# PEER selection of the dense tokens stretched over the first products, and gathered rows of v 128 rounds behind those of u instead of 40

## What is computed

```python
q = (xb @ w_q).reshape(blk, PEER_HEADS, 2, PEER_HALF)          # 8 heads, two halves of 128
s = jnp.einsum('thcd,hcnd->thcn', q, sub_keys)                 # 128 keys for each half
s_top, i_top = lax.top_k(s, PEER_TOPK)                         # 16 best of each half
cand_s = (s_top[:, :, 0, :, None] + s_top[:, :, 1, None, :])   # 256 pairs
best_s, best_pos = lax.top_k(cand_s, PEER_TOPK)                # 16 best pairs = 16 experts
expert = jnp.take_along_axis(cand_e, best_pos, axis=-1)        # of 128 * 128
gate = jax.nn.softmax(best_s, axis=-1)
act = jax.nn.gelu(jnp.einsum('td,thkd->thk', xb, u[expert]))
return jnp.einsum('thk,thkd->td', gate * act, v[expert])
```

## Time and profile before

| what | us |
|---|---|
| runs of the kernel | 5276.35 median of 3 (5275.28 to 5283.59) |
| the profiled execution | 5254.98 |
| its span in the trace | 5253.1 |
| PEER of layer 0, gathers 1044 to 2476, first stage until | 1843 |
| its one-hot stage | 1843 to 1996 |
| its third stage, with the last gathers | 1996 to 2476 |
| PEER of layer 1, first stage until | 4585 |

### The profile page before, as it was taken

The page is one execution under the profiler, slowest core; times in us unless marked ns, Lnnn a source line. Parts: engine busy times, 40 slices in busy tenths (PEclk is TensorE's granted clock), DMA queues, the critical chain, the costliest instruction groups (busy, mean ns, idle before and its releaser), DMA issues. The chain is left out here.

```text
span 5253.1 us, 56097 instructions
## 1 busy us (share of the span) xinstructions
PE 4308.1 (82%) x21158; PEld 3533.7 (67%) x21158; DVE 3096.9 (59%) x5685; ACT 1026.1 (20%) x2272; POOL 1920.2 (37%) x1559
## 2 busy tenths in 40 slices
PE   6989679788997559996787799996888997469995
PEld 5467438577886458885555688863677886458884
DVE  1315540599957796656216633345599867796656
ACT  0102310222332150000012222211222332150000
POOL 0000230166657624444002433312256557614444
PEclk9985669899998779998878788858899998779997
DMA  2330112488889948998111000013588889939998
GB/s 91 89 75 1 34 37 96 167 301 313 311 338 397 369 128 342 409 396 348 56 58 35 1 1 1 1 41 104 188 300 310 319 341 390 363 109 371 409 399 333
DMA packets 403487, 1099.26 MB, mean 209 GB/s; under 512 B 70508, under 2 KB 157261, under 8 KB 402886
## 3 DMA queue, kind: packets, MB, share of 16 engines
q0 software_dynamic: 186496, 679.04, 34.4%
q1 hardware_dynamic: 216726, 416.69, 22.6%
HBM read 1066.88 MB, written 32.45 MB: 209 GB/s over the span
## 5 line engine op out<-in xcount | busy, mean ns | idle before, releaser
L1036 DVE SCALAR_TENSOR_TENSOR gg_ytok<-gg_ring,gg_gw,gg_ytok 128x1024 f32<-128x1024 f32 x320 | 422.1, 1319 | 178.5 <-DMA gg_ring<-in_peer_v,gg_idx 172.5
L1036 DVE SCALAR_TENSOR_TENSOR fg_ytok<-fg_ring,fg_gw,fg_ytok 128x1024 f32<-128x1024 f32 x320 | 422.0, 1319 | 176.6 <-DMA fg_ring<-in_peer_v,fg_idx 170.0
L706 POOL DMA_INDIRECT fg_ring<-in_peer_u,fg_idx x320 | 377.2, 1179 | 351.7 <-DVE fg_ring L1030 284.4
L706 POOL DMA_INDIRECT gg_ring<-in_peer_u,gg_idx x320 | 374.4, 1170 | 345.7 <-DVE gg_ring L1030 275.9
L1030 DVE SCALAR_TENSOR_TENSOR fg_ring<-fg_ring,fg_htok 128x1024 f32<-128x1024 f32 x320 | 409.7, 1285 | 128.1 <-DMA fg_ring<-in_peer_u,fg_idx 126.4
L1030 DVE SCALAR_TENSOR_TENSOR gg_ring<-gg_ring,gg_htok 128x1024 f32<-128x1024 f32 x320 | 409.8, 1286 | 127.8 <-DMA gg_ring<-in_peer_u,gg_idx 125.7
L774 PE MATMUL fg_bank<-f_hTd,fg_uT 128*128 128x256 f32 x2048 | 476.9, 387 | 0.6 <-ACT f_buf L873 0.6
L774 PE MATMUL gg_bank<-g_hTd,gg_uT 128*128 128x256 f32 x2048 | 476.2, 387 | 0.6 <-ACT g_buf L873 0.6
L706 POOL DMA_INDIRECT gg_ring<-in_peer_v,gg_idx x320 | 358.1, 1119 | 272.1 <-DVE gg_ytok L1036 211.8
L706 POOL DMA_INDIRECT fg_ring<-in_peer_v,fg_idx x320 | 345.7, 1080 | 276.3 <-DVE fg_ytok L1036 214.4
L774 PEld LDWEIGHTS fg_bank<-f_hTd,fg_uT 128*128 128x128 f32 x2048 | 389.8, 196 | 51.2 <-issue 0.9
(11 more groups left out here) (620 smaller groups left out, 7758.8 us busy)
## 6 DMA issues: line engine op xcount, KB each, us to landing
fg_ub<-in_peer_u SPq DMA_DIRECT2D x128, 512.0 KB, 6.8
gg_ub<-in_peer_u SPq DMA_DIRECT2D x128, 512.0 KB, 6.7
fg_ub<-in_peer_v SPq DMA_DIRECT2D x64, 512.0 KB, 7.2
fg_uT<-in_peer_v SPq DMA_DIRECT2D x64, 512.0 KB, 6.7
gg_ub<-in_peer_v SPq DMA_DIRECT2D x64, 512.0 KB, 7.3
gg_uT<-in_peer_v SPq DMA_DIRECT2D x64, 512.0 KB, 6.8
f_buf<-in_peer_w_q SPq DMA_DIRECT2D x16, 1024.0 KB, 12.2
g_buf<-in_peer_w_q SPq DMA_DIRECT2D x16, 1024.0 KB, 11.8
```

Source lines behind the costliest of these rows:

```text
L706: pool.indirect_dma_start(ring[:, n % RING, :], None, (u_rows if kind == "u" else v_rows)[:, :], bass.IndirectOffsetOnAxis(ap=idx[:, r:r + ...
L1036: dve.scalar_tensor_tensor(ytok[:, :], row, gw[:, r:r + 1], ytok[:, :], ALU.mult, ALU.add).then_inc(used, 1)
```

## The change

Passes 4 to 7, those of the dense tokens, now have 55, 55, 55 and 30 units between their steps and 18, 18, 18 and 14 blocks beside them, so that 263 of the 370 units of the first stage lie among selection steps instead of 172, and 97 of the 128 blocks instead of 65. `LAG` goes from 40 to 128 (`SLOTS`). The selection buffers are laid out in the order in which they come free, and ACT's one wait at block 79 becomes five, at blocks 79 (queries multiplied), 95 (last scores), 108, 113 and 118 (picked). The margin for the dots' Gelus goes from 25 to 40. No instruction of the computation is added or removed.

```diff
-LAG = 40
+LAG = SLOTS
-UNITS_SEL = (0, 20, 24, 24, 26, 26, 26, 26)
-BLOCKS_SEL = (3, 8, 9, 9, 9, 9, 9, 9)
+UNITS_SEL = (0, 20, 24, 24, 55, 55, 55, 30)
+BLOCKS_SEL = (3, 8, 9, 9, 18, 18, 18, 14)
-HTR_AT = 16640
+HTR_AT = 17664
...
-        for c, k in zip(early_chunks, place(sched, [dots_at[c] for c in early_chunks], 25.0)):
+        for c, k in zip(early_chunks, place(sched, [dots_at[c] for c in early_chunks], 40.0)):
...
-                        if b == lim_end:
-                            act.wait_ge(gate_done, npass)
+                        if b == lim_w:
+                            act.wait_ge(mm_done, 4 * npass)
+                        if b == lim_q:
+                            act.wait_ge(sc_done, npass)
+                        if b == lim_s:
+                            act.wait_ge(s_used, npass)
+                        if b == lim_rest:
+                            act.wait_ge(off_done, npass)
+                        if b == lim_hit:
                             act.wait_ge(idx_done, npass)
```

More of the change, by code:

```diff
@@ L474, in top_of_buf @@
             return buf[:, free[0]:free[0] + n]
+        hit = top_of_buf(10 * TOPK * TOPK).rearrange("p (a e i j) -> p a e i j", a=2, e=5, i=TOPK)
+        lim_hit = free[0] // TD
+        s_rest = top_of_buf(10 * P).rearrange("p (e c n) -> p e c n", e=5, c=2)
+        lim_rest = free[0] // TD
+        s_sb = top_of_buf(10 * P).rearrange("p (e c n) -> p e c n", e=5, c=2)
+        lim_s = free[0] // TD
+        qT = top_of_buf(4 * TR).rearrange("p (h c t) -> p h c t", h=2, c=2)
         keysT = top_of_buf(HC * P).rearrange("p (h n) -> p h n", n=P)
+        lim_q = free[0] // TD
         wt = top_of_buf(4 * D).rearrange("p (b k n) -> p b k n", b=2, k=KD)
[L478 to L482, removed]
+        lim_w = free[0] // TD
         lim_a = HTR_AT // TD
@@ L563, in peer_layer @@
             if p + 1 < npass:
+                assert nb <= lim_w, (nb, lim_w)
                 some_queries(p + 1)
@@ L567, in peer_layer @@
                 assert nb <= lim_a, (nb, lim_a)
-        assert nb <= lim_end, (nb, lim_end)
         some_blocks(nblk - nb)
```

## The result

The changed kernel took 5246.51 us (median of 4 runs, 5242.55 to 5251.9), the kernel before 5277.24 in the runs beside it (4 runs). The ratio is 0.9947, interval 0.9925 to 0.9968: faster by 31 us, more than the 10.5 us that the prediction took as what can be told from no change, and less than half of the 66 that were forecast.

The account below looks back on a forecast made before the run. DMA was taken to bind the first stage once selection is stretched; -44 + 6 + 5 = -33 us a layer, -66 for two layers, takes 5276.35 to 5210 us, range 5165 to 5262.

Parts of the forecast that it names:

- share 0.95 from the beginning of pass 4: First stage, layer f: DMA share 0.95 or more from 1217 us on would show the forecast right.
- a sign against itself: Passes of the first stage: DMA share below 0.9 would say that unused DMA time had not become used.
- The term of -44: First stage: with selection stretched, DMA binds and the stage ends at 1799 instead of 1843, 44 us less a layer.
- the lower bound of 17: First stage: gain of only 17 us if 218 MB go at 358 GB/s, taking 609 us.
- The first rival: First stage: the mix stays at the passes' rate, gains 17 us, -6 a layer after the exchange, 5264 us; chance 0.17.
- fast mix: First stage: the mix goes at the third stage's 401 GB/s, gains 82 us, 71 a layer net, 5134 us; chance 0.09.
- the full queue without holes: First stage from pass 4: 582 us of full queue at share 1.02 take 570 us, before 12 us for mask holes.
- slower: One-hot and third stages: ytok exchange costs 15 and 11 us, first stage gains at most 17; 5294 us; chance 0.05.
- No change: Selection steps: DVE waits for late scores or exponentials, 23 or 46 us a layer; within some 20 of 5276; chance 0.05.
- +6 and +5: Exchange of ytok between neighbouring units of v: DVE's stops add 6 us to the one-hot stage, 5 to the third.
- The exponential and ACT's five waits: First stage: DVE's 22.8 us wait for the last pass's exponential goes; ACT's five waits cost 0.
- the step from "DMA unused" to "DMA used": First stage: what it can gain is what its DMA leaves unused, so 582 us of full queue sets its length.

Follow-up runs that it names:

- mask cut: The changed kernel, but POOL multiplies only a sixteenth of the mask in the four dense passes, so work is left out: 5226.26 us, ratio 0.9887.
- the last experiment: Changed kernel with ring of seven, units behind all seven steps, lag 116: 5143.86 us; from it, mask halves apart: 5140.79 us; mask mostly left out: 5139.9 us.

## Why the prediction was off

*What bounds the stage.* Right for what binds afterwards: DMA share is 0.95 over the stage, DVE's waits moved into the passes, and TensorE ended 51 us ahead of DVE. Of the signs that the prediction named, share 0.95 from the beginning of pass 4 came out at 0.95 for the stage, but under 0.9 in pass 7, which it had put down as a sign against itself. TensorE took 553 us from the beginning of pass 4, 508 without its waits of 45; the prediction had 530 and 510.

*The term of -44.* This is the step that failed: "a pass still has holes ... Half of 6.53 in each of four passes is 12 us". Measured are -19.4 and -22.2, near the lower bound of 17 and not the value. The queue lay open for 42 us, and 39 of them lie in the passes (40 in layer g), as many as the 35 and 40 of before. The prediction read the open queue in the passes of before as "DVE is nearly always busy", which units moved in between would use, and counted only the stretch in which POOL works on something else, the mask. It overlooked that DVE stops freeing places whenever it carries out steps: 8.4 us at the beginning of each pass, and shorter steps between. Six gathers cover most of that but not all, and the queue then needs another ten microseconds to fill. These holes belong to the steps, and the stretch puts more units between the steps but leaves as many steps as there were. The row was at hand: in the kernel before, too, POOL stood with six gathers out at the beginning of pass 5 (first row below). What the stretch did close lies behind the passes, 22 us before and 3 after, and some 16 of these 22 are the stretch around DVE's wait for the last exponential (second row, of before).

```profile
1290.09 1.74 POOL L706 DMA_INDIRECT fg_ring<-in_peer_u,fg_idx  x1 [7.68 <-DVE fg_ring L1030]
...
1472.00:1502.00 30.00, 30.00 (x168) 26.81 (x167) 7.15 (x11) 13.05 (x25) 4.25 (x4) 1.00 0.49 154
```

After, the first 22 us of each of the four passes, and 14 us from the beginning of each product of the mask:

```profile
1236.50:1258.50 22.00, 22.00 (x122) 19.64 (x121) 18.75 (x63) 10.17 (x19) 11.96 (x10) 0.99 0.82 273
1358.40:1380.40 22.00, 22.00 (x125) 19.66 (x124) 18.96 (x59) 7.76 (x17) 11.15 (x9) 1.00 0.88 322
1474.90:1496.90 22.00, 22.00 (x123) 19.65 (x122) 19.06 (x57) 7.40 (x16) 11.59 (x10) 1.00 0.92 338
1588.80:1610.80 22.00, 22.00 (x124) 19.48 (x123) 21.79 (x83) 7.70 (x18) 8.61 (x8) 1.00 0.87 322
...
1334.30:1348.30 14.00, 14.00 (x79) 12.48 (x78) 13.59 (x15) 4.46 (x10) 12.60 (x7) 1.00 0.69 226
1453.20:1467.20 14.00, 14.00 (x78) 12.51 (x77) 13.72 (x11) 7.11 (x12) 12.63 (x7) 1.00 0.83 297
1566.70:1580.70 14.00, 14.00 (x75) 12.37 (x75) 13.46 (x13) 4.30 (x10) 12.62 (x7) 0.95 0.69 247
1645.50:1659.50 14.00, 14.00 (x64) 11.96 (x64) 13.96 (x13) 2.99 (x7) 11.40 (x7) 0.84 0.65 224
```

The open time of a stretch is its length less share times length divided by 1.02. For layer f, with unrounded shares:

| open queue, us | stage | beginnings | behind masks | elsewhere in the passes | behind the passes |
|---|---|---|---|---|---|
| before (its passes not divided) | 57 | – | – | 35 | 22 |
| after | 42 | 13 | 17 | 9 | 3 |
| mask cut | 35 | 13 | 8 | 10 | 4 |
| units behind all steps | 37 | 2 | 18 | 11 | 6 |
| seven places | 29 | 8 | 11 | 8 | 2 |
| seven places, all steps, lag 116 | 28 | 1 | 12 | 6 | 9 |

So the beginnings, which the prediction put at nothing, are 13 us, the masks 17 instead of 12, and other places in the passes 9. The experiments carry this: units behind all steps close the beginnings and are worth 9 us, the cut of the mask closes half of its hole and is worth 7 to 9, and a seventh place is worth 21 (13 of it in share, the rest in more GB/s for the same share: 358 / 0.95 = 377 against 370 / 0.97 = 381; why the same bytes take less of the queue's time with seven places is not shown). The gains do not simply add up: with places and steps together the stage is 568 to 576 us, and a further cut of the mask moves the time to another wait.

*The first rival*, the mix at the rate of the passes, had the size of the first stage nearly right (a gain of 17, and 5264 us in all), but not the cause. The mean of the first stage after is 358 GB/s (604.8 us at share 0.95), and the Trainium skill, "DMA: Bandwidth & Descriptors", Specifications, has about 358 GB/s as a core's limit from HBM. Here that is a coincidence: inside this stage are stretches at 395 and 404, the third stage goes at 399, and one place more in the ring lifts the same stage to 370, with the two other edits to 375. The *fast mix* (share as in the third stage) was not reached by any kernel; the best, at 568 to 576 us, stands where the full queue without holes was put, 570, but by luck: its queue is still open for some 28 us in layer f, and the same bytes take less of the queue's time. The *slower* rival had its stops at their contended prices: in the one-hot stage that did not occur, and in the third stage, where it did (16.4 us below), only a part of it reached the length. *No change*, by waits for exponentials, did not occur after; such a wait came back in the kernel with seven places, all steps and lag 116 (14.8 us in layer f), which kept the entries on ACT at estimated times.

*The exchange of ytok.* +6 and +5 forecast; +5.7 and +3.5, +2.6 and +3.6 measured. In order of time on POOL and DVE in the one-hot stage, a wait of DVE in the same stage, and two of the third:

```profile
1907.56 0.57 POOL L683 DMA_DIRECT2D scratch_xs<-fg_ytok  x1 [3.45 <-DVE fg_ytok L1047]
1910.78 0.56 POOL L679 DMA_DIRECT2D fg_ytok<-scratch_xs  x1 [2.64 <-DMA scratch_xs<-fg_ytok]
...
1914.56 1.28 DVE L1047 SCALAR_TENSOR_TENSOR fg_ytok<-fg_ring,fg_gw,fg_ytok 128x1024 f32<-128x1024 f32 x1 [3.81 <-issue]
...
DVE f_buf L1065 <- PE fg_bank L804: 9.8, 10, 4.0
...
DVE fg_ytok L1032 <- DMA scratch_xs<-fg_ytok: 10.8, 1, 10.8
DVE fg_ytok L1047 <- issue: 5.6, 1, 5.6
```

In the one-hot stage store and load took 7.0 us in all (10.3 estimated) and DVE stood 3.81 (6.6 estimated); with 2.7 us more of waits for the gates (9.8 against 7.1) that is about the 5.7 measured. In the third stage DVE stood for 16.4 us (15 estimated), and a quarter to a third of the additional 11 came through; that gathers land in the meantime would do this, but is not shown by itself. Mechanism and place were right, as the stretch alone shows, where with the old lag the one-hot stage is 155.6. That +6 was met so well is in part luck, since DVE's stop was smaller than estimated and the waits for the gates, which the sum did not have, made up for it.

*The exponential and ACT's five waits.* Right at 22.8 us gone and at no cost: ACT's waits for DVE in front of an exponential, 11.1 and 4.0 us, stood under TensorE's spare time. What the prediction did not see is how much of the gain this is: the open queue around the wait, some 16 us, is most of what the stage lost in open time (57 to 42). No run takes the wait away alone, so its share is read from the trace and not shown by an experiment. In the three kernels of the last experiment the layer with the longer wait has the longer first stage, by 7 to 14 us for 12 to 18 us of wait.

So the bound and the exchange were right, and the step from "DMA unused" to "DMA used", as the prediction calls it, was not: the holes of the passes, put at 12 us, are 39 and did not shrink. In the sum, -44 should have been -21, and the -33 a layer about -10; the stages measured -11 and -15, and the medians, with 31 us for two layers, a little more.

## What to carry to other kernels

Before a bound is put at "share 1.0", divide the ring by the rate at which it is used up, and compare that time with every piece of work in which the consumer frees no place: the hole appears behind such a piece, and lasts until the queue has been filled again. More work between the same pieces dilutes such holes but leaves them as many as they were. Where consumer and queue are near balance, spread the consumer's other work over as many places as there are and buy one more buffer before moving work about; here the two, with the shorter lag, brought another 1.9% where the stretch and the lag alone had brought 0.5%. And the price of a place is found by taking it away as well as by adding it, since it grows quickly below the balance.

## What was not expected of the hardware

- One buffer of 512 KB is worth 42 to 49 us of a 604 us stage from five to six, and 21 from six to seven; the stage with six places runs at 358 GB/s on the average, with five at 333 and with seven at 370, for the same bytes.
- A store of 512 KB out of the core's memory with POOL's wait for it was over in 3.2 us in the one-hot stage (DMA share 0.42), and made DVE wait 10.8 us in the third (share 1.01); from issue to landing the four stores of after took 2.9 to 10.2 us.
- The two units beside POOL's product take 3.4 us instead of 1.2, one after the other, each about as long as one of the product's two halves. The Trainium skill, "SBUF — State Buffer", Who interferes with whom, says that a VectorE instruction with two inputs in SBUF contends with a GpSimd instruction that reads SBUF, and that the port pair the two share is an exclusive lock; the rows agree (3.38 and 3.37 beside 6.56 for both halves), and DVE's busy time falls by 16 us when the product is cut.
